# Gated-delta and mLSTM phase of a hybrid encoder: norms in the gate exponents, masks on TensorE, the out projection in 32 pieces

## The reference, cut to what matters

```python
q = _l2_normalize(q) * 128 ** -0.5;  k = _l2_normalize(k)         # DeltaNet
decay = where(incl, exp(g_i - g_j), 0)
L = where(strict, (k * beta) @ k.T * decay, 0)
u, w = solve(eye + L, [v * beta, k * beta * exp(g)])
o = (q * exp(g)) @ S + (q @ k.T * decay) @ (u - w @ S)
S = S * exp(g_last) + (k * exp(g_last - g)).T @ (u - w @ S)
w = exp(log_w - m_t) * (q @ k.T)                                  # mLSTM
h = (w @ v) / max(abs(sum(w)), exp(-m_t))
y = rms_norm(o, norm_g) * gate;   h = h + concat(y_rw, y_gd, y_ml) @ w_out
```

## Time and profile before

| | |
|---|---|
| median of three runs | 3178.85 us |
| profiled execution: span, first to last instruction | 3174.6 us |
| TensorE busy, share | 3054.9 us, 96% |
| VectorE busy | 2081.5 us, 66% |
| ScalarE busy | 1657.2 us, 52% |
| GpSimd busy | 612.3 us, 19% |
| mean granted TensorE clock | 0.978 of 2.4 GHz |
| the changed phase, three passes and the turning behind them | 227.2 us per layer |

### The profile page before, as it was taken

How to read it: one execution, slowest core, us unless ns; L and a number is a source line. 1 busy time by engine, 2 the same in 40 slices (tenths; PEclk the granted TensorE clock), 3 DMA queues, 4 the chain that set the end, 5 groups by cost and what they waited for, 6 DMA issues and landing times.

```text
span 3174.6 us, 56293 instructions
## 1 busy us (share of the span) xinstructions
PE 3054.9 (96%) x20767; PEld 2626.2 (83%) x20767; DVE 2081.5 (66%) x3474; ACT 1657.2 (52%) x2673; POOL 612.3 (19%) x517
## 2 busy tenths in 40 slices
PE   8999988899999999999999999889899999999998
PEld 7899877777888888888788998777688888888886
DVE  6775655777777777455568655567767777774554
ACT  6555654456555555444455556545465555544444
POOL 2000453440212222000000005334402221220000
PEclk9999998999999999999999999999899999999999
DMA  6666101114656666666556660021256665666664
GB/s 208 185 180 187 47 2 59 61 55 146 195 185 192 192 182 196 221 195 191 164 169 194 183 178 15 2 66 55 67 178 193 184 192 181 196 198 215 193 183 152
DMA packets 265227, 479.22 MB, mean 151 GB/s; under 512 B 17314, under 2 KB 81148, under 8 KB 264380
## 3 DMA queue, kind: packets, MB, share of 16 engines
q1 hardware_dynamic: 265020, 476.48, 49.1%
HBM read 474.32 MB, written 2.10 MB: 150 GB/s over the span
## 4 chain that ended last, share of the span: by engine, by line
PE 87%; DVE 8%; ACT 1%; issue 1%; DVEq 1%; POOL 0%; SPq 0%; DMA 0%; ACTq 0%; POOLq 0%
PE ps L643 86%; PE ps L647 1%; DVE scores L2194 1%; DVE wlo L1801 1%; DVE XS L1851 0%; ACT L1272 0%; DVE upair L1814 0%; DVE TN L1860 0%; DVE AR L2221 0%; DVE H L1833 0%; ACT XS L1272 0%; DVE st L1875 0%; DVE TN L2246 0%; DVE heads L1880 0%; POOL H L580 0%
## 5 line engine op out<-in xcount | busy, mean ns | idle before, releaser
L1801 DVE TENSOR_TENSOR wlo<-ring,whi 128x1024 fp32r<-128x1024 f32 (+4 forms) x905 | 1095.6, 1229 | 672.2 <-ACT whi L1272 666.3
L643 PE MATMUL ps<-upair,whi 128*128 128x512 f32 x4032 | 1404.4, 394 | 6.3 <-DVE upair L1814 5.7
L1272 ACT ACTIVATE whi<-ring 128x1024 fp32r<-128x1024 f32 (+4 forms) x947 | 941.0, 1002 | 795.6 <-PE ps L643 715.8
L643 PE MATMUL ps<-upair,wlo 128*128 128x256 f32 x4032 | 1121.2, 278 | 0.0
L643 PEld LDWEIGHTS ps<-upair,whi 128*128 128x128 f32 x4032 | 756.5, 188 | 182.9 <-issue 6.1
L643 PEld LDWEIGHTS ps<-upair,wlo 128*128 128x128 f32 x4032 | 758.9, 188 | 0.3 <-issue 0.2
L643 PE MATMUL ps<-whi,upair 128*128 128x390 f32 (+2 forms) x1280 | 367.5, 364 | 0.0
L625 POOL TENSOR_TENSOR YB<-YB 128x1024 f32<-128x1024 f32 x22 | 125.3, 5697 | 828.9 <-DVE YB L1824 828.9
L643 PE MATMUL ps<-whi,ghi 128*128 128x512 f32 x704 | 274.4, 390 | 0.0
L643 PE MATMUL ps<-whi,glo 128*128 128x512 f32 x704 | 274.0, 389 | 0.0
L643 PE MATMUL ps<-wlo,ghi 128*128 128x512 f32 x704 | 273.9, 389 | 0.0
(11 more groups left out here) (311 smaller groups left out, 3621.5 us busy)
## 6 DMA issues: line engine op xcount, KB each, us to landing
ring<-in_w_up_dram SPq DMA_DIRECT2D x352, 512.0 KB, 3.9
ring<-in_w_down_dram SPq DMA_DIRECT2D x176, 512.0 KB, 4.3
ring<-in_w_in_dram SPq DMA_DIRECT2D x128, 384.0 KB, 3.5
ring<-in_w_out_dram SPq DMA_DIRECT2D x64, 512.0 KB, 3.7
ring<-in_w_ple_gate_dram SPq DMA_DIRECT2D x64, 512.0 KB, 4.4
ring<-in_w_in_dram SPq DMA_DIRECT2D x51, 512.0 KB, 4.5
ring<-in_w_in_dram SPq DMA_DIRECT2D x64, 390.0 KB, 3.5
ring<-in_w_in_dram SPq DMA_DIRECT2D x32, 396.0 KB, 3.6
```

Source lines behind the costliest of these rows:

```text
L643: return pe.matmul(o_, a, b, start=start, stop=stop, skip_group_check=True)
L1272: return act.activation(o_, i_, f, **kw)
L1801: v.tensor_tensor(wlo[:, slot % RING, :, 0:w], ring[:, slot % RING, :, 0:w], whi[:, slot % RING, :, 0:w].bitcast(F32), SUB).then_inc(S["lo ...
```

## The change

The norms of q and k leave the operands. GpSimd squares q and k (`gd_squares`) during the RWKV pairs, TensorE sums them over channels as columns (`gd_sums`), ScalarE takes their logs, and VectorE adds -1/2 of them to the cumulative gates, so that one exponential gives decay and norm. Raw q and k are then the operands. The masks are added in PSUM by one bfloat16 product per decay group, -2^100 times a 0/1 mask (`far`, `beyond`), and ScalarE's Exp reads PSUM with the gate as bias; VectorE's subtraction and GpSimd's masking of the DeltaNet decays go. The scaled values and keys come from ScalarE's copy out of PSUM with a scale (VS, OT). GpSimd multiplies the head gains into the gates once per layer (`gains_into_gates`) and copies the mLSTM values (`values_with_ones`); the mLSTM differences are ScalarE's Relu with bias. `heads_out` is one operation of three operands per tile. Both families share one root per pass. The mLSTM gate rows move into the last RWKV pair (`ml_rows_begun`, `ml_rows_ended`). The output projection goes in 32 pieces of one product (three matmuls): one ahead of each of the four groups of levels 1 to 5, the other twelve spread over the tail; `turn_out` moves into level 0, the PSUM copies are done in halves. The load of ml_norm_g moves from the output projection to the second block of the input projection.

The diff, cut and with its indentation reduced:

```diff
-OUT_BANKS = ((1, 5), (1, 5), (1, 5), (2, 6))
+OUT_BANKS = (1, 5)
+PIECES = 4 * OUT_SLOTS
...
+sel(upto[d][:], one_h[:], ALU.is_ge, 0, [[step, P]], cm)
+sel(far[:], far[:], ALU.not_equal, 0, [[-1, P]], 1, -2.0 ** 100)
...
+    for j in range(2):
+        z = zgd[:, GH * j + 2 * i:GH * j + 2 * i + 2, :]
+        last = pool.tensor_tensor(gsq[:, 2 * j:2 * j + 2, :], z, z, ALU.mult)
...
+    zg = third(zgt[:, t, heads3], 3)
+    pool.tensor_tensor(zg, zg, bmid(gdn[:, :], 3), ALU.mult)
+    zm = zmt[:, t, MW + half * 3 * P:MW + half * 3 * P + 3 * P]
+    pool.tensor_tensor(zm, zm, mln[:, heads3], ALU.mult).then_inc(S["gd_gate"], 1)
...
+    values_with_ones(i)
+    pool.wait_ge(S["inv_tn1"], pool.snap(L * (2 * (RC + GP)) + (i * 2 + 2 * RC)) + 2)
+    if i:
+        split_lo(sg, SL_OUT)
+        split_lo(sg, SL_OUT + 1)
+        add_partial(ng, -2)
+        split_lo(sg, SL_OUT + 2)
+    split_lo(sg, SL_OUT + 3)
+    ml_masks(0)
+    if i:
+        add_partial(ng, -1)
+    ml_masks(1)
+    split_lo(sg, SL_OUT + 4)
+    add_partial(ng, 0)
+    split_lo(sg, SL_OUT + 5)
     split_lo(sg, SL_OUT + 6)
     split_lo(sg, SL_OUT + 7)
     add_partial(ng, 1)
...
+    def gd_sums():
+        pe.wait_ge(S["gd_sq"], L * GP + c)
+        if more:
+            pe.wait_ge(S["rw_rn"], n + 2)
+        for k in range(4):
+            for t in range(NT):
+                last = mm(ps[1][:, T + NT * k + t:T + NT * k + t + 1], gsq[:, k, t * P:(t + 1) * P], ones[:, 0:1],
+                          True, True)
+        last.then_inc(S["gd_ssq"], 1)
+
     hooks = {0: output_scores, 1: keys_turned, 4: early_values}
...
+    def busy_beside_sums():
+        if c:
+            pe.wait_ge(S["gd_ssqc"], L * GP + c)
+        keep_quarters_busy(1)
...
-def out_slot(g, s, banks=OUT_BANKS):
+def out_piece(g, n):
+    i, r = divmod(n, 8)
+    t, q = divmod(r, 4)
+    j, kk = divmod(q, KS)
+    slot = SL_OUT + OUT_SLOTS * g + 2 * i + j
+    c = KS * j + kk
...
+    if i and q == 0:
+        pe.wait_ge(S["wo_evac"], L * (2 * GP * NO) + (2 * NO * g + 2 * (i - 1) + t + 1))
+    if t == 0 and kk == 0:
+        slot_wait(base, slot)
+    last = product(ps[OUT_BANKS[t]][:, :], (yhi[:, c, t * P:(t + 1) * P], ylo[:, c, t * P:(t + 1) * P]),
+                   wparts(slot, kk, 0, 512), q == 0, q == 3)
+    if t == 0 and q == 3:
+        last.then_inc(S["wo_half"], 1)
+    if t == 1 and kk == 1:
+        last.then_inc(S["slot_done"], 1)
...
+def decays(i, d, j):
+    bank = ps[2 + d] if j else ps[4 * d]
+    mm(bank[:, :], far[:, :], bmid(beyond[d][j], 4), True, False)
+    for h in range(2):
+        for t in range(NT):
+            u = 2 * h + t
+            last = mm(bank[:, u * P:(u + 1) * P], gate_of(5 if j else 0, t, d, 2 * i + h).to_broadcast([P, P]), ident[:],
+                      False, u == 3)
+    last.then_inc(S["gd_gb"], 1)
+
+def key_scores(i):
+    for h in range(2):
+        for t in range(NT):
+            tok = slice(t * P, (t + 1) * P)
+            last = mm(ps[6 + h][:, t * T:(t + 1) * T], zgd[:, GH + 2 * i + h, tok],
+                      zgd[:, 2 * i + h:2 * i + h + GH + 1:GH, tok], True, True)
+    last.then_inc(S["gd_sc"], 1)
...
-            last = turn(ps[3][:, (2 * h + t) * P:(2 * h + t + 1) * P], AR[h][:, t, 0, :])
-    last.then_inc(S["gd_kt"], 1)
-    out_slot(i, 0)
+    values_turned(i, n4)
     def before_t():
         pe.wait_ge(S["gd_vtc"], n + 1)
         pe.wait_ge(S["gd_ktc"], n + 1)
-
-    invert(m2, lambda d, j: scores[d][:, 2, j, :], {lv: lambda lv=lv: ml_pair(n, n2, lv) for lv in (1, 2, 4, 5)},
-           {(0, "x", 1): lambda: out_slot(i, 1), (0, "t", 0): before_t, (2, "t", 0): lambda: out_slot(i, 2),
-            (LEV - 2, "t", 0): lambda: out_slot(i, 3), (LEV - 1, "t", 0): lambda: out_slot(i, 4)})
-    out_slot(i, 5)
+        turn_out(i)
+
+    inside = {(0, "t", 0): before_t}
+    for lv in range(1, LEV):
+        for p, where in enumerate((("x", 0), ("x", 1), ("t", 0), ("t", 1))):
+            inside[lv, *where] = lambda piece=4 * (lv - 1) + p: out_piece(i, piece)
+    invert(m2, lambda d, j: scores[d][:, 2, j, :],
+           {lv: lambda stage=stage: ml_pair(i, n, n2, stage) for lv, stage in ((0, 1), (2, 2), (4, 4))}, inside)
+    used = 4 * (LEV - 1)
...
+    ml_pair(i, n, n2, 5)
+    for d in range(2):
         pe.wait_ge(S["gd_uf"], n2 + (d + 1))
         for h in range(2):
...
+    out_pieces(i, used, used + 2)
+    pe.wait_ge(S["ml_numc"], n2 + 2)
...
+    out_pieces(i, used + 2, used + 4)
...
+    if i < GP - 1:
+        pe.wait_ge(S["gd_q"], n2 + 2)
+        key_scores(i + 1)
+    out_pieces(i, used + 4, used + 6)
...
+    last.then_inc(S["gd_y"], 1)
     if i < GP - 1:
-        pe.wait_ge(S["wo_evac"], L * (GP * NO) + (NO * (i + 1) - 1))
-        squared_sums(pe.snap(n + 1), (1, 5))
-    for s in range(6, OUT_SLOTS):
-        out_slot(i, s)
+        for d in range(2):
+            decays(i + 1, d, 0)
+        decays(i + 1, 0, 1)
+    out_pieces(i, used + 6, used + 8)
+    if i < GP - 1:
+        pe.wait_ge(S["gd_yc"], n + 1)
+        decays(i + 1, 1, 1)
+    out_pieces(i, used + 8, PIECES)
...
+            for j in range(NT):
+                last = a(ml_flat(d)[:, h, j, :], ps[4 * d + 3][:, h * T:(h + 1) * T], ACT.Relu,
+                         bias=mflat[:, 2 * d + j, 2 * i + h:2 * i + h + 1])
...
-def partial_out(ng, sg, i):
-    act.wait_ge(S["wo_added"], ng + (i - 1))
-    act.wait_ge(S["slot_done"], sg + (RING + SL_OUT + 2 * i + 2))
-    for t in range(NT):
-        last = a(partial[i % 2][:, t, :], ps[OUT_BANKS[i][t]][:, :], ACT.Copy)
-    last.then_inc(S["wo_evac"], 1)
...
+def decays(i, d, j):
+    act.wait_ge(S["gd_gb"], L * (4 * GP) + (4 * i + 2 * j + d + 1))
+    for h in range(2):
+        for t in range(NT):
+            u = 2 * h + t
+            last = a(scores[d][:, j, u, :], (ps[2 + d] if j else ps[4 * d])[:, u * P:(u + 1) * P], ACT.Exp,
+                     bias=gate_of(6, t, d, 2 * i + h))
+    last.then_inc(S["gd_dm"], 1)
...
-    a(mono(Vt, 4), ps[2][:, :], ACT.Copy).then_inc(S["gd_vtc"], 1)
+    for d in range(2):
+        for h in range(2):
+            for t in range(NT):
+                u = 2 * h + t
+                last = a(VS[d][:, u, :], ps[2][:, u * P:(u + 1) * P], ACT.Copy, scale=gate_of(1, t, d, 2 * i + h))
+    last.then_inc(S["gd_vtc"], 1)
...
+    for d in range(2):
+        act.wait_ge(S["gd_u"], n2 + (d + 1))
+        a(mono(ufg[d], 2), ps[4 * d][:, 0:T], ACT.Copy).then_inc(S["gd_uf"], 1)
+    partial_out(i, ng, sg, 2, 0)
...
+    partial_out(i, ng, sg, 2, 1)
+    split_out(sg, lg, 9)
+    for d in range(2):
+        act.wait_ge(S["gd_us"], n2 + (d + 1))
+        a(mono(KBt[d][:, :, :], 2), ps[4 * d][:, T:2 * T], ACT.Copy, scale=-1.0).then_inc(S["gd_usc"], 1)
+    if i < GP - 1:
         for d in range(2):
-            act.wait_ge(S[src], n2 + (d + 1))
-            a(mono(dst[d][:, :, :], 2), ps[4 * d][:, lo:lo + T], ACT.Copy).then_inc(S[done], 1)
-    split_out(sg, lg, 9)
+            decays(i + 1, d, 0)
+        decays(i + 1, 0, 1)
+    partial_out(i, ng, sg, 3, 0)
+    if i < GP - 1:
+        decays(i + 1, 1, 1)
     ready_logs()
-    if i < GP - 1:
-        square_logs(act.snap(n + 1))
...
+    a(st[:, 1:3, :], st[:, 1:3, :], ACT.Exp, scale=-0.5).then_inc(S["gd_rstd"], 1)
     split_out(sg, lg, 10)
+    partial_out(i, ng, sg, 3, 1)
...
+        for t in range(NT):
+            lnq, lnk = both_directions(0, t), both_directions(1, t)
+            for row, src, ln, op in ((0, 0, lnk, ADD), (4, 4, lnk, ADD), (6, 2, lnk, SUB), (5, 2, lnq, ADD)):
+                last = v.scalar_tensor_tensor(by_direction(row, t), ln, -0.5, by_direction(src, t), MUL, op)
+        last.then_inc(S["gd_cumc"], 1)
...
+def ml_rows_begun():
+    v.wait_ge(S["ml_rt"], L + 1)
+    for d in range(2):
+        v.tensor_copy(lf_r[:, d * T:(d + 1) * T], ps[4 * d + 3][0:MH, T:2 * T])
+    v.drain()
+    for o_, i_ in zip(halves(F_r), halves(lf_r)):
+        v.tensor_tensor_scan(o_, i_, i_, 0.0, ADD, ALU.bypass)
+    v.drain()
+    for d in range(2):
+        half = slice(d * T, (d + 1) * T)
+        v.tensor_tensor(e_rows[:, half], ps[4 * d + 3][0:MH, 0:T], F_r[:, half], SUB)
+    v.drain()
+
+def ml_rows_ended():
+    for o_, i_ in zip(halves(M_r), halves(e_rows)):
+        v.tensor_tensor_scan(o_, i_, i_, 0.0, MAX, ALU.bypass)
+    v.drain()
+    for d in range(2):
+        v.tensor_copy(mrow[d], M_r[:, d * T:(d + 1) * T])
+    v.tensor_tensor(m_rows, F_r, M_r, ADD).then_inc(S["ml_rows"], 1)
...
+def heads_out(i):
+    v.wait_ge(S["gd_rstd"], L * GP + i + 1)
+    if i == 0:
+        v.wait_ge(S["gd_gate"], L * RC + RC)
+    for k, (o, gate, col) in enumerate(((OL, zmt[:, :, MW:2 * MW], RW + GW), (Vt, zgt[:, :, 0:GW], RW))):
+        for h in range(2):
+            for t in range(NT):
+                u = 2 * h + t
+                cols = slice(i * T + h * P, i * T + (h + 1) * P)
+                last = v.scalar_tensor_tensor(YB[:, t, col + i * T + h * P:col + i * T + (h + 1) * P], o[:, u, :],
```

(46 more changed lines are left out.)

528 lines of the change are left out of this document (206 added, 322 removed).

## The result

The kernel after takes 3239.99 us (median of four runs, 3232.39 to 3251.55), the kernel before beside it 3182.45 (four runs, 3176.93 to 3188.97): a ratio of 1.0188, interval 1.0160 to 1.0216. The change makes the kernel 1.9% slower. The forecast was 3170, in a range of 3130 to 3205, and faster. The profiled execution has a span of 3242.4 us against 3174.6. That is 67.8 more, where the medians differ by 57.5 (executions of the kernel after differ by up to 19 us), so the loss stands inside the trace.

What follows compares the result with a forecast made beforehand. The chain was taken as 87% TensorE, 8% VectorE. Per layer -8.2 (passes 1, 2), -1.0 (pass 0), -1.7 (exit), +5.8 (RWKV), +1.0 (gains' DMA) = -4.1; two layers -8.2: 3166.4, plus 4.3 outside the span, 3170; range 3130 to 3205.

Steps and rivals of the forecast that it cites:

- low clock behind a wait of 4 us: After TensorE's wait before turning YB: 3.4 us lost per pass to low clock, no second fall; bounds 0 to 12.
- column sums: Sums of squares in RWKV pairs 1 to 3: 1.7 us each in pairs 1 and 2, free in pair 3.
- stretch 1: From T, a pass's last output product (pass 0: last RWKV product), to YB's turning: T+15.2, T+18.3 in pass 0, ScalarE last.
- The list of what would show me wrong: Pieces at 0.69 throughout, low clock reaching level 3, GpSimd's low parts holding a piece, or TensorE's pre-turning wait over 6 us.
- RWKV part: Added costs in the RWKV pairs, from sums, gate operations, mLSTM rows and shared VectorE access: +5.8 us, bounds +2 to +9.
- Rival (c): ScalarE's in-order queue in stretch 1 ends later than added up; 3.5 us more a pass gives 3191. Chance 0.12.
- Rival (a): Change of operand hides between short pieces, so a piece costs 3 x 0.23; 23 us less in all, 3147. Chance 0.26.
- Stretch 2: From level 0's second products to level 5, with turning and 20 pieces added: 38.1 us a pass.
- rival (b): Low clock lasts over levels 1 and 2, losing 11.4 us instead of 3.4 a pass: 3218. Chance 0.13.
- Stretch 3: From the inversion to a pass's last output product, with six pieces and mLSTM work moved in: 14.3 us.
- The exit: Behind the last pass, from last output product to TensorE's turning: 7.2 us instead of 8.9, so -1.7.
- Rival (d): The change removes only covered work, so only the RWKV part moves: +13, 3192. Chance 0.04.

Runs made afterwards that it cites:

- e1: Kernel after, with GpSimd's low parts and adding made to wait until heads_out is done in passes 1 and 2: 3206.54 us, 1.0090 of before.
- e2: Kernel after, with 640 bytes of small tiles moved behind the arena, which so starts at 120704 as before the change: 3229.06 us, 1.0143 of before.
- e3: Kernel before, with only the arena and all behind it 640 bytes higher, at 121344: 3198.14 us, 1.0052 of before.
- e5: Kernel e1, with unread 512-column bf16 products on TensorE while it waits to turn YB: 3197.05 us, 1.0042 of before.
- e4: Kernel after, with one column-sum product instead of eight, leaving out the norms of q and k: 3223.85 us, 1.0132 of before.
- e11: Kernel after, with two unused 128x1024 GpSimd multiplications starting beside the last heads_out of each layer: 3251.52 us, 1.0217 of before.
- e7: Kernel e1, with each level's four output pieces together ahead of the level's first product: 3188.00 us, 1.0019 of before.
- e9: Kernel e7, with the busy products of e5 and the arena moved back as in e2: 3170.49 us, 0.9961 of before.
- e8: Kernel before, with the arena 512 bytes higher, at 121216: 3182.32 us, 0.9996 of before.
- e12: Kernel e9, with column sums of RWKV pairs 1 and 2 replacing the eight unread products at the pair's end: 3166.65 us, 0.9927 of before.

## Why the prediction was wrong

By the ratio the miss is 68 us: 60 of loss (0.0188 of 3182) and 8 of gain that did not come. It divides like this. What each part took beyond its forecast, 31, 14 to 17, 11 and 11, sums to 67 to 70. The parts are from experiments, the low clock from the windows of the traces; that they add is assumed, and each difference of two ratios is uncertain by some 10 us:

| | forecast | measured |
|---|---|---|
| head outputs held by GpSimd | 0 | 31 (e1) |
| start of the arena | 0 | 14 to 17 (e2, e3) |
| low clock behind a wait of 4 us, four passes | 14 (4 x 3.4) | 25 (4 x 6.3, half of the 12.7 us worked at the low level); 16 come back in e5 |
| column sums | 7 | 18 (e4) |

**The step that failed** is in stretch 1: "the reciprocal roots at T+10.5, eight products of heads_out (0.26) to T+12.6". The roots were there at T+10.3 and the products began at T+10.4. They took 11.07 us, 1.4 each, not 2.1 in all: GpSimd's five long operations held them. I took 0.26 from a quiet place and never asked what GpSimd does at that moment. The diff shows it: GpSimd's `split_lo` of slots 0 and 1 and `add_partial` wait for `inv_tn1`, the start of the inversion, and `heads_out` was moved behind that start. Before, the order was the other way round, so the same wait kept the two apart. The list of what would show me wrong named GpSimd's low parts, but as something that holds up a piece, and the wait over 6 us, but without a cause: what decides was beside VectorE, not ahead of TensorE.

The trace of the kernel before had already shown the price. VectorE's product of q or k with its norms (AR, two operands in SBUF) takes 0.41 us, but 2.62 where a long GpSimd operation starts with it. VectorE, then GpSimd:

```profile
576.33 2.62 DVE L2221 SCALAR_TENSOR_TENSOR AR<-Z,UA 128x256 f32<-128x256 f32 x1
...
579.20 0.41 DVE L2221 SCALAR_TENSOR_TENSOR AR<-Z,UA 128x256 f32<-128x256 f32 x1
```

```profile
576.30 2.36 POOL L574 TENSOR_TENSOR wlo<-ring,whi 128x1024 fp32r<-128x1024 f32 x1 [19.02 <-DVE st L1875]
```

It is so in passes 1 and 2 of both layers, 4 of the 12 operations of that line; the other eight take 0.41.

The Trainium skill, "SBUF — State Buffer", section "Who interferes with whom", says that a VectorE instruction with two SBUF inputs contends with a GpSimd instruction that reads SBUF, and that the port pair they share is an exclusive lock. The trace agrees: `heads_out` reads heads and Z, its longest instruction took 2499 ns, about one whole GpSimd operation (2.40), its shortest 340, and in e11 two such operations added 4.3 us.

What it is worth can be worked out from rows: the roots are ready at 594.6, GpSimd's run ends at 604.8, and with ScalarE done at 599.1 TensorE loses 6.9 of its start (605.98) a pass, 27 in the four; e1 gave back 27 in the traces of these passes, 31 by the ratio. I had allowed 0.4 for it, in the RWKV part, and nothing here.

Point by point:

- *ScalarE ends stretch 1 at T+15.2, pass 0 at T+18.3.* Right: T+14.96 once GpSimd is out of the way, and 18.3 in pass 0 of the kernel after (530.21 from 511.89), which turns the RWKV outputs and has no `heads_out` ahead of it. Rival (c), a later ScalarE, is out.
- *A piece is 0.88.* Right: 0.90 for a piece at the full clock. Rival (a), free changes of operand, is out, and e7 shows the price of pieces that stand alone: 0.76 a level.
- *Stretch 2 is 38.1.* It was 43.5 in pass 1 and 40.3 in pass 0. In pass 1 the clock lost 6.3, not 3.4, which is 2.9 of the 5.4; levels at the full clock took 6.02 rather than 5.7.
- *The low clock: 3.4 us lost a pass, ending in level 1.* It does end in level 1 (618.6), so rival (b), which has levels 1 and 2 at the low level, is out. The term was mis-sized, and not only by the 11 us: after the forecast wait of 4.2 (e1) TensorE still worked 12.3 us at the low level, not 6, as the turning, the small products and the broadcast ahead of level 1 alone take 7.5 us there. I had taken the six from a stretch with whole slots behind it.
- *Stretch 3 is 14.3.* Right: 13.7. *The exit is 1.7 shorter:* 1.3, as it took 9.1 before, not 8.9, and takes 7.8, not 7.2.
- *RWKV part: +5.8, bounds 2 to 9.* Pairs 1 to 3 are 9.9 longer (1.9 of it is a turning moved in from behind them). 16 records at 0.12 were counted rightly. Not counted was that the clock can fall behind them. Seven traces have the sums of pairs 1 and 2 at this place with nothing between them (after, e1, e2, e5, e7, e9, e11): in 16 of their 28 pairs the clock falls, and such a pair takes 37.2 to 39.1 us; the others take 35.9 to 36.2. In the traces of before, e3, e8 and e4 it falls in none of 16 (34.0 to 34.7), in e12 in none of 4. "They may even keep the clock", said of pair 3, did not come: the low stretch there is 10.2 us, as before, and a second one of 3.4 follows. In pair 3, moved mLSTM rows gave a wait of 1.60 us for VectorE:

```profile
504.67 0.49 PE L686 MATMUL ps<-XS,odd_ar 128*128 128x128 f32 x2 [1.60 <-DVE XS L2210]
```

- *The address:* no term of the sum, and none could have come from the profile of before. It is the part that only an experiment shows.
- *Rival (d), only covered work goes:* out. With all four mended passes 1 and 2 are 7.2 and 8.8 us shorter.

Open: which divisor of 512 decides the address effect (only remainders 384 and 0 were run). Why a remainder slows the products is open too. The clock behind the sums falls in some pairs and not in others of the same kernel, and I can't say what decides. Why the pieces in fours (e7) keep the clock better was not separated from their shorter time.
